# Routing of a product-key expert layer: three buffers of one-hots, GpSimd gates eight batches of sixteen in full, VectorE the last one of the last search

## The reference, cut to what matters

```python
q = (xb @ w_query).reshape(tb, PEER_HEADS, 2, PEER_HALF)
s = jnp.einsum('thpc,hpnc->thpn', q, sub_keys)
top_s, top_i = lax.top_k(s, PEER_TOPK)
cand_s = top_s[:, :, 0, :, None] + top_s[:, :, 1, None, :]      # 16 x 16 a head
best_s, best_pos = lax.top_k(cand_s, PEER_TOPK)
idx = jnp.take_along_axis(cand_i, best_pos, axis=-1)            # expert = high * 128 + low
g = jax.nn.softmax(best_s, axis=-1)
u = expert_u[idx]
h = gelu(einsum('thkd,td->thk', u, xb))
out = einsum('thk,thkd->td', g * h, expert_v[idx])
```

## Time and profile before

| | us |
|---|---|
| median of 3 runs | 2833.64 (2833.35 to 2840.89) |
| profiled execution, whole | 2833.43 |
| its span, first to last instruction | 2831.6 |
| PE busy | 2593.4 (92%) |
| DVE busy | 2270.7 (80%) |
| ACT busy | 922.9 (33%) |
| POOL busy | 1283.2 (45%) |

### The profile page before, as it was taken

How to read it: one execution, slowest core, us unless ns; L and a number is a source line. 1 busy time by engine, 2 the same in 40 slices (tenths; PEclk the granted TensorE clock), 3 DMA queues, 4 the chain that set the end, 5 groups by cost and what they waited for, 6 DMA issues and landing times.

```text
span 2831.6 us, 47150 instructions
## 1 busy us (share of the span) xinstructions
PE 2593.4 (92%) x17256; PEld 1704.5 (60%) x17459; DVE 2270.7 (80%) x4538; ACT 922.9 (33%) x1604; POOL 1283.2 (45%) x865
## 2 busy tenths in 40 slices
PE   8999978999867745899999999999999999999996
PEld 3566645679867744565565665665665665665653
DVE  4244555658999998688988988888988988988988
ACT  3333334531035546332222232232332332332324
POOL 2110010010044441456765666666666766766762
PEclk9999998999979865999999999999999999999998
DMA  4000203330012245999999999999999999999995
GB/s 162 23 16 16 75 8 119 133 114 2 1 42 115 115 182 214 347 370 363 350 364 343 350 364 344 340 356 361 344 358 348 341 354 366 331 364 362 343 321 217
DMA packets 274155, 682.16 MB, mean 241 GB/s; under 512 B 29464, under 2 KB 111896, under 8 KB 269728
## 3 DMA queue, kind: packets, MB, share of 16 engines
q0 software_dynamic: 110592, 402.70, 38.3%
q1 hardware_dynamic: 163360, 276.73, 27.5%
HBM read 622.73 MB, written 56.62 MB: 240 GB/s over the span
## 4 chain that ended last, share of the span: by engine, by line
PE 55%; issue 8%; DVE 8%; POOL 4%; DMA 2%; ACT 1%; DVEq 0%; POOLq 0%; ACTq 0%; SPq 0%
PE o_psum L2002 27%; PE h_psum L1991 26%; POOL rt_hot L1280 3%; PE r_t_psum L1116 2%; DVE wide L1844 1%; DMA early<-u_blocks 1%; DVE rt_hot L1496 1%; DVE rt_hot L1486 1%; DVE rt_top_u L1331 1%; DMA early<-v_blocks,pick_index 1%; DVE rt_top L1329 0%; DVE rt_pos L1371 0%; POOL rt_cand L1264 0%; DVE wide L1943 0%; DVE wide L1832 0%
## 5 line engine op out<-in xcount | busy, mean ns | idle before, releaser
L1991 PE MATMUL h_psum<-early 128*128 128x384 bf16 (+1 forms) x6144 | 856.9, 300 | 7.0 <-DVE early L1810 4.8
L2002 PE MATMUL o_psum<-v_split,w_split 128*128 128x512 bf16 x3681 | 820.7, 379 | 11.2 <-DVE v_split L1817 1.7
L1991 PEld LDWEIGHTS h_psum<-early 128*128 128x128 bf16 x6144 | 601.5, 98 | 261.9 <-issue 8.8
L2002 PEld LDWEIGHTS o_psum<-v_split,w_split 128*128 128x128 bf16 x3840 | 375.6, 98 | 436.3 <-DVE v_split L1817 2.1
L1555 POOL DMA_INDIRECT early<-u_rows,pick_index x320 | 440.3, 1376 | 274.8 <-DVE dots L1840 198.8
L1555 POOL DMA_INDIRECT early<-v_blocks,pick_index x320 | 455.6, 1424 | 231.0 <-DVE wide L1844 146.3
L1844 DVE SCALAR_TENSOR_TENSOR wide<-early,dots,wide 128x1024 f32<-128x1024 f32 x320 | 405.8, 1282 | 17.8 <-DMA early<-v_blocks,pick_index 15.6
L1840 DVE CUSTOM_DVE_ANT_0 early<-early,wide 128x1024 f32<-128x1024 f32 x320 | 386.2, 1221 | 8.5 <-DMA early<-u_rows,pick_index 8.1
L1704 ACT ACTIVATE act_out<-h_psum 128x384 f32<-128x384 f32 (+1 forms) x256 | 97.9, 435 | 621.7 <-PE h_psum L1991 569.2
L1712 ACT ACTIVATE v_split<-early 128x512 bf16<-128x512 f32 x256 | 160.4, 627 | 353.5 <-PE o_psum L2002 342.5
L1116 PE MATMUL r_t_psum<-x_t,early 128*128 128x128 f32 (+1 forms) x1920 | 233.5, 283 | 0.0
(11 more groups left out here) (218 smaller groups left out, 2932.5 us busy)
## 6 DMA issues: line engine op xcount, KB each, us to landing
early<-u_blocks SPq DMA_DIRECT2D x128, 512.0 KB
early<-v_blocks SPq DMA_DIRECT2D x256, 256.0 KB
gates<-wide SPq DMA_DIRECT2D x20, 2048.0 KB, 6.4
gate<-gates SPq DMA_DIRECT2D x32, 1280.0 KB
early<-w_query SPq DMA_DIRECT2D x8, 1024.0 KB, 5.6
early<-w_fox SPq DMA_DIRECT2D x4, 1536.0 KB, 6.4
early<-u_rows,pick_index POOLq DMA_INDIRECT x320
early<-v_blocks,pick_index POOLq DMA_INDIRECT x320
```

The lines of the kernel that those rows point to most:

```text
L1991: mm = pe.matmul(h_psum[:, half, 0:width * P], u_split[:, q % 2, part, c], xs[:, first:first + width, xpart, c, :], start=(c == 0 and part ...
L2002: mm = pe.matmul(o_psum[t][:, :], w_split[:, w_slot(r, q), part, t * P:(t + 1) * P], v_split[:, k, vpart], start=(q == 0 and part + vpart ...
```

## The change

The number of one-hot buffers becomes three. A batch's buffer is m % 3, only batch 15 has buffer 1, so that batch 0 of the next search can have buffer 0 (`HOT_SLOT`); VectorE waits for the batch that last used its buffer (`HOT_USED`: three batches back for most, two for batches 1 and 15, four for 0 and 2). GpSimd multiplies both parts for batches 0, 1, 2, 4, 5, 7, 8 and 15; no batch is shared. VectorE multiplies both parts for batches 3, 6 and 9 to 14. In search 3 (DENSE - 2) batch 15 is VectorE's too; search 4 is all VectorE's, as before. Because of this exception GpSimd's and VectorE's loops end one step earlier and step 4 is written out.

```diff
@@ -1044,7 +1044,7 @@
         keys_t = sb("keys_t", [P, P // 8, 2, 8], BF16)
         gates_t = sb("gates_t", [P, P // 8, 2, 8], BF16)
         gate_t = sb("gate_t", [P, P])
-        HOTS = 2
+        HOTS = 3
         BATCH = 8
 
         hot = sb("hot", [P, HOTS, 4, BATCH // 2, N_KEYS, 2], BF16)
@@ -1060,13 +1060,24 @@
         hot_made, hot_by_pool, summed_gates, g_copied = sem("hot_made"), sem("hot_by_pool"), sem("summed_gates"), sem("g_copied")
         SLOTS = P // BATCH
 
-        POOL_BOTH, POOL_LOW = (0, 1, 2, 15), (4, 5, 6, 7, 8)
-        POOL_SLOTS = tuple(sorted(POOL_BOTH + POOL_LOW))
-        DVE_SLOTS = tuple(m for m in range(SLOTS) if m not in POOL_BOTH)
-
-        def shared(d):
-
-            return not (isinstance(d, int) and d == DENSE - 1)
+        POOL_SLOTS = (0, 1, 2, 4, 5, 7, 8, 15)
+        DVE_SLOTS = tuple(m for m in range(SLOTS) if m not in POOL_SLOTS)
+        HOT_SLOT = tuple(m % HOTS for m in range(SLOTS - 1)) + (1,)
+        HOT_USED = tuple(min(k for k in range(1, SLOTS) if HOT_SLOT[(m - k) % SLOTS] == HOT_SLOT[m])
+                         for m in range(SLOTS))
+        FREE = 4
+
+        def by_pool(d, m):
+
+            return m in POOL_SLOTS and not (isinstance(d, int) and (d == DENSE - 1 or (d == DENSE - 2 and m == SLOTS - 1)))
+
+        def dve_before(d, m):
+
+            if isinstance(d, int) and d == DENSE - 1:
+                return len(DVE_SLOTS) * d + 1 + m
+            if isinstance(d, int) and d == DENSE - 2 and m == SLOTS - 1:
+                return len(DVE_SLOTS) * (d + 1)
+            return len(DVE_SLOTS) * d + DVE_SLOTS.index(m)
 
         def by_pair(row):
 
@@ -1138,18 +1149,16 @@
 
                 def gate_batch(d, m):
                     n = SLOTS * d + m
-                    if m in POOL_SLOTS and shared(d):
+                    if by_pool(d, m):
                         pe.wait_ge(hot_by_pool, len(POOL_SLOTS) * d + POOL_SLOTS.index(m) + 1)
-                    if not shared(d):
-                        pe.wait_ge(hot_made, len(DVE_SLOTS) * d + m + 1)
-                    elif m in DVE_SLOTS:
-                        pe.wait_ge(hot_made, len(DVE_SLOTS) * d + DVE_SLOTS.index(m) + 1)
+                    else:
+                        pe.wait_ge(hot_made, dve_before(d, m) + 1)
                     for four in range(BATCH // 4):
                         pe.wait_ge(g_copied, 2 * n + four + 1)
                         for j in range(4 * four, 4 * four + 4):
                             for part in range(2):
-                                mm = pe.matmul(g_psum[four % 2][:, j % 4], hot[:, m % HOTS, 1, j // 2, :, j % 2],
-                                               hot[:, m % HOTS, 2 + part, j // 2, :, j % 2],
+                                mm = pe.matmul(g_psum[four % 2][:, j % 4], hot[:, HOT_SLOT[m], 1, j // 2, :, j % 2],
+                                               hot[:, HOT_SLOT[m], 2 + part, j // 2, :, j % 2],
                                                start=(part == 0), stop=(part == 1))
                         mm.then_inc(summed_gates, 1)
 
@@ -1170,7 +1179,7 @@
 
 
 
-                pe.sem_inc(summed_gates, 2 * HOTS)
+                pe.sem_inc(summed_gates, 2 * FREE)
                 pe.sem_inc(g_copied, 2)
                 pe.sem_inc(picks_turned, 1)
                 for t in range(GATHERED + 2):
@@ -1215,7 +1224,7 @@
                     for four in range(2):
                         token = (BATCH * m + 4 * four) % CHUNK
                         chunk, k = BATCH * m // CHUNK, BATCH * m // CHUNK % 2
-                        act.wait_ge(summed_gates, 2 * (SLOTS * d + m) + four + 1 + 2 * HOTS)
+                        act.wait_ge(summed_gates, 2 * (SLOTS * d + m) + four + 1 + 2 * FREE)
                         if token == 0:
 
                             act.wait_ge(stage_stored[k], 16 * (CHUNKS // 2 * d + chunk // 2 + 1))
@@ -1275,14 +1284,12 @@
 
                 def gate_batch(d, m):
 
-                    n, slot, first = SLOTS * d + m, m % HOTS, 0 if m in POOL_BOTH else 1
-                    pool.wait_ge(high_made, n + 1)
-                    pool.tensor_tensor(hot[:, slot, 2 + first:4],
-                                       hot[:, slot, 0].unsqueeze(1).broadcast_to(
-                                           [P, 2 - first, BATCH // 2, N_KEYS, 2]),
-                                       by_pair(gates_t[:, m, first:2].rearrange("p k n -> p (k n)")).rearrange(
-                                           "p (k j) n two -> p k j n two", k=2 - first), ALU.mult
-                                       ).then_inc(hot_by_pool, 1)
+                    slot = HOT_SLOT[m]
+                    pool.wait_ge(high_made, SLOTS * d + m + 1)
+                    pool.tensor_tensor(hot[:, slot, 2:4],
+                                       hot[:, slot, 0].unsqueeze(1).broadcast_to([P, 2, BATCH // 2, N_KEYS, 2]),
+                                       by_pair(gates_t[:, m].rearrange("p k n -> p (k n)")).rearrange(
+                                           "p (k j) n two -> p k j n two", k=2), ALU.mult).then_inc(hot_by_pool, 1)
 
                 def step(d):
                     t = d + GATHERED
@@ -1297,15 +1304,16 @@
                                 products(t)
                             if m == PRODUCTS_SLOT - 2:
                                 float_index(t)
-                        if m in POOL_SLOTS and shared(d - 1):
+                        if by_pool(d - 1, m):
                             gate_batch(d - 1, m)
 
                 pool.sem_inc(floated, 1)
                 for t in range(GATHERED + 1):
                     products(t)
                     float_index(t)
-                with pool.Fori(1, DENSE) as d:
+                with pool.Fori(1, DENSE - 1) as d:
                     step(d)
+                step(DENSE - 1)
                 step(DENSE)
                 pool.wait_ge(q_done, 4 * TILES)
                 pool.wait_ge(kept, GATHERED)
@@ -1479,24 +1487,23 @@
                     dve.wait_ge(kept, t + 1)
 
                 def one_hots(d, m):
-                    n, slot = SLOTS * d + m, m % HOTS
+                    n, slot = SLOTS * d + m, HOT_SLOT[m]
                     if m == 0:
                         dve.wait_ge(picks_copied, d + 1)
-                    dve.wait_ge(summed_gates, 2 * n + 2)
+                    dve.wait_ge(summed_gates, 2 * (n - HOT_USED[m] + 1 + FREE))
                     dve.tensor_tensor(hot[:, slot, 0:2].rearrange("p k j n two -> p (k j) n two"),
                                       key_table[:, :, :].unsqueeze(1).broadcast_to([P, BATCH, N_KEYS, 2]),
                                       by_pair(keys_t[:, m].rearrange("p k n -> p (k n)")), ALU.is_equal
                                       ).then_inc(high_made, 1)
-                    if m in POOL_BOTH and shared(d):
+                    if by_pool(d, m):
                         return
-                    halves = 1 if m in POOL_LOW and shared(d) else 2
                     dve.wait_ge(high_made, n + 1)
                     if m in (0, DVE_SLOTS[0]):
                         dve.wait_ge(gate_split, d + 1)
-                    dve.tensor_tensor(hot[:, slot, 2:2 + halves],
-                                      hot[:, slot, 0].unsqueeze(1).broadcast_to([P, halves, BATCH // 2, N_KEYS, 2]),
-                                      by_pair(gates_t[:, m, 0:halves].rearrange("p k n -> p (k n)")).rearrange(
-                                          "p (k j) n two -> p k j n two", k=halves), ALU.mult).then_inc(hot_made, 1)
+                    dve.tensor_tensor(hot[:, slot, 2:4],
+                                      hot[:, slot, 0].unsqueeze(1).broadcast_to([P, 2, BATCH // 2, N_KEYS, 2]),
+                                      by_pair(gates_t[:, m].rearrange("p k n -> p (k n)")).rearrange(
+                                          "p (k j) n two -> p k j n two", k=2), ALU.mult).then_inc(hot_made, 1)
 
                 dve.tensor_copy(key_table[:, :, :], iota.unsqueeze(2).broadcast_to([P, N_KEYS, 2])
                                 ).then_inc(table_made, 1)
@@ -1510,12 +1517,16 @@
                         pick(t, slot, 1)
                     if t < GATHERED:
                         keep_picks(t)
-                with dve.Fori(1, DENSE) as d:
+                def step(d):
                     pick(d + GATHERED, 0, d + 1)
                     for slot in range(SLOTS):
                         if slot + 1 < SLOTS:
                             pick(d + GATHERED, slot + 1, d + 1)
                         one_hots(d - 1, slot)
+
+                with dve.Fori(1, DENSE - 1) as d:
+                    step(d)
+                step(DENSE - 1)
                 for slot in range(SLOTS):
                     one_hots(DENSE - 1, slot)
```

## The result

The changed kernel takes 2855.59 us (median of 6 runs, 2850.08 to 2856.79), the one before 2837.93 (median of 6, 2833.35 to 2840.89): a ratio of 1.0059, 95% interval 1.0048 to 1.0069. It is slower by 0.59%; forecast were 2850.3 us and +16.9 (0.6%).

What follows compares the result with a forecast made beforehand. VectorE's queue was taken to bound routing steps 1 to 4. +19.3 us for four steps less 2.4 for batch 15 made +16.9 on 2833.43, so 2850.3 us; own range 2845 to 2856, wider range 2841 to 2862.

Steps and rivals of the forecast that it cites:

- VectorE sets the pace of steps 1 to 4, TensorE doesn't: Routing steps 1 to 4: the length of VectorE's queue alone decides the time, 71.36 us a step before.
- rival 2: Routing steps 1 to 3: TensorE becomes the bound as its clock falls in new gaps, +5 a step, 2865 us; chance 0.07.
- The wait lasts until GpSimd's end, however long: One-hots of batches 5, 6, 8, 9: blocked until GpSimd's 3.60 us instruction ends, four new waits, +7.74 us a step.
- rival 1: Those one-hots: GpSimd's long instruction lets VectorE through, waits at most 0.54 us; 2828.0, or 2819.3 without loss; chance 0.11.
- Batches 4 to 9: VectorE's queue in each of four steps: new waits less gates handed over, +4.83 us a step, +19.3 in all.
- Third buffer: One-hot buffers in routing: VectorE never waited for one, so a third takes off 0 us.
- Batch 15 of search 3: End of step 4, before the tail: gated by VectorE, the tail comes 2.43 us earlier; bounds 2.4 gained or nothing.
- Step 4 written out: VectorE's and GpSimd's loops ending a step earlier: cost 0, bounds 0 to 1 us.
- From stretch to time: Whole kernel: +16.9 us added to the profiled execution's 2833.43 gives 2850.3, the median taken as within noise of it.

Runs made afterwards that it cites:

- e2: Changed kernel, but GpSimd multiplies only 512 of 2048 gate elements in batches 4, 5, 7 and 8, the rest left out; ratio 0.9946 to the kernel before.
- e1: Changed kernel with two one-hot buffers instead of three; ratio 1.0056 to the kernel before.
- e8: Kernel before with three one-hot buffers and batch 15 of search 3 VectorE's; first to last one-hot 318.47 us (before 321.29), one run.
- e5: Changed kernel with batch 15 of search 3 given back to GpSimd; first to last one-hot 340.24 us (changed kernel 337.86), one run.
- e4: Kernel before with only batch 15 of search 3 made VectorE's, step 4 written out; ratio 0.9987 to the kernel before.
- e3: Changed kernel with GpSimd's instruction in batches 4, 5, 7 and 8 cut into four of 512 elements; ratio 1.0031 to the kernel before.
- e7: Kernel before with batches 2 and 4 to 9 shared by halves and batch 15 of search 3 VectorE's; ratio 1.0003 to the kernel before.

## Why the prediction was right

- *VectorE sets the pace of steps 1 to 4, TensorE doesn't.* Right: in the changed kernel's stretch with one-hots VectorE never waits for TensorE, and rival 2 fell. The new gaps on TensorE came (2.54 us before batch 7's sums), and the granted clock was 0.92 and 0.91 at 921 to 941, but it was 0.84 at 921 to 931 before, and TensorE's slack took the gaps up (TensorE's timeline and the busy times by stretch of the changed kernel):

```profile
929.82 1.89 PE L1160 MATMUL g_psum<-rt_hot 128*128 128x128 bf16 x16 [2.54 <-POOL rt_hot L1289]
```

```profile
921.00:931.00 10.00, 7.46 (x82) 7.26 (x80) 9.96 (x32) 5.18 (x7) 3.77 (x2) 0.92 0.00 0
931.00:941.00 10.00, 9.52 (x95) 9.28 (x93) 9.71 (x27) 6.31 (x7) 3.44 (x1) 0.91 0.50 210
```

- *The wait lasts until GpSimd's end, however long.* Right. Forecast 3.43 and 2.88 us for the held one-hots, measured 3.42 and 2.87; rival 1 (a wait capped near 0.54) is excluded by these rows and by e2. The one row that carried this was outside the part of the program that was changed, a 5.7 us wait in attention; the routing's own waits ended at 0.57 (the longest one-hot took 1.79 us, 0.03 more than the prediction's longest). The 5.7 takes L453's own length as 1.2 us, which the earlier trace rows doesn't show, since L453 runs once; the three TENSOR_TENSORs of 1024 f32 elements behind it take 1.19 to 1.23 and bear it out.
- *Batches 4 to 9: +4.83 a step.* Steps went from 71.17, 71.36, 71.36 to 76.00, 76.22, 76.10: +4.83, +4.86, +4.74. The fourth, which is written out, went from 71.10 to 73.24 up to the tail: +2.14, or +4.55 with the 2.41 of batch 15 put back.
- *Third buffer: nothing.* e1 and e8.
- *Batch 15 of search 3: -2.43.* 8.51 to 6.10 is -2.41; e5 gives 2.38 by itself.
- *Step 4 written out: 0.* The size was off by a little: the bounds were 0 to 1, and what came lies below 0. e4 and the changed kernel both have some 0.3 to 0.4 us less there than the other terms give (+16.57 against 19.28 - 2.43 = 16.85 in the changed kernel, -2.87 against -2.43 in e4).
- *From stretch to time.* Forecast +16.9 from the profiled execution; the stretch gave +16.6, the medians +17.7, since the six runs of each kernel are spread over the two levels of the attention phase differently. I took the run-to-run spread as noise of 0.2 us by the two runs nearest the median; it has two levels 5 to 6 us apart, which the 2840.89 already showed, and that is why 2850.3 is 5 us under the median while the difference is right within 1. The forecast was worked out from an execution of the lower level, and the changed kernel's one run there took 2850.08. That the median, 2855.59, still lies inside the forecast's own range of 2845 to 2856 is in part luck: it does so by 0.4 us, and the range left no room for the level.

## What to carry to other kernels

## What the runs showed of the hardware that I had not expected

- Small copies and scalar operations with one input are held as well, until GpSimd's instruction ends: 0.16 to 0.22 us become 1.02 to 1.92 (e3, e7).
- Cutting GpSimd's 3.60 us into four pieces of 1.03 helps by 1.7 us a step only: pieces and VectorE's instructions take turns, so each small instruction behind can be held by a piece of its own, and gates that come later keep buffers in use.
- The granted clock in the attention phase, 1.00 or 0.59 at 320 to 330 us with the same program ahead of it, goes with 5.5 us on a whole execution, a third of what was to be measured. The same code repeats in the trace to some 0.02 us a step (71.17 and 71.36 for the first two steps of the kernel before, 71.16 and 71.35 for e4's), and stretches that differ in the third buffer alone to 0.05 and 0.14 us, where the medians' interval for the change is 6 us wide.
